# A two-layer encoder on one core: reciprocals moved in the second attention's steps, and a third token chunk of 344 columns

## The reference

```
for i in range(DEPTH):
    u = rmsnorm(h, norm_mix[i])
    mix = neighbourhood_attention(...) if kind == 0 else gqa_attention(...)
    h = h + mix
    h = h + swiglu(rmsnorm(h, norm_ffn[i]), ffn_w1[i], ffn_w3[i], ffn_w2[i])
return rmsnorm(h, norm_final)[:, N_META:]
```

## Time and profile before

| what | us |
|---|---|
| median of 3 runs (2755.27, 2755.56, 2759.28) | 2755.56 |
| the profiled execution, device time | 2760.81 |
| its span, first to last instruction | 2758.9 |
| TensorE busy in the span | 2688.9 (97%) |
| VectorE busy | 1497.9 (54%) |
| GpSimd busy | 1525.8 (55%) |
| ScalarE busy | 943.2 (34%) |
| mean granted TensorE clock | 0.993 of 2.4 GHz |

### The profile page before, as it was taken

How to read it: one execution, slowest core, us unless ns; L and a number is a source line. 1 busy time by engine, 2 the same in 40 slices (tenths; PEclk the granted TensorE clock), 3 DMA queues, 4 the chain that set the end, 5 groups by cost and what they waited for, 6 DMA issues and landing times.

```text
span 2758.9 us, 39747 instructions
## 1 busy us (share of the span) xinstructions
PE 2688.9 (97%) x14623; PEld 2209.2 (80%) x14623; DVE 1497.9 (54%) x1962; ACT 943.2 (34%) x1630; POOL 1525.8 (55%) x1291
## 2 busy tenths in 40 slices
PE   8999999899999999999999899999998999999998
PEld 7888888699999999999777444454677888888886
DVE  4444444437444444445877866767356444545545
ACT  4343343324222222223321546554232222222224
POOL 5655655445655555556344657665445555655561
PEclk9999999999999999999999999999999999999999
DMA  7221221511111111111333000001211111112111
GB/s 225 64 60 57 61 71 46 206 43 54 57 50 49 46 46 46 46 49 54 103 82 62 19 1 16 16 1 62 89 46 54 46 57 49 49 54 59 51 54 65
DMA packets 200468, 163.06 MB, mean 59 GB/s; under 512 B 19816, under 2 KB 182032, under 8 KB 200352
## 3 DMA queue, kind: packets, MB, share of 16 engines
q1 hardware_dynamic: 193728, 139.83, 17.5%
q10 hardware_dynamic: 6624, 21.68, 2.0%
HBM read 131.70 MB, written 24.51 MB: 57 GB/s over the span
## 4 chain that ended last, share of the span: by engine, by line
PE 67%; issue 11%; POOL 11%; DVE 8%; DMA 1%; ACT 1%; SPq 1%; POOLq 0%; ACTq 0%; DVEq 0%
PE PS L984 17%; PE PS L916 11%; PE PS L1035 11%; PE PS L1180 9%; POOL wl L701 6%; PE PS L1454 4%; PE PS L1468 4%; POOL upraw L695 3%; PE PS L1231 2%; DVE nmx L2530 2%; PE PS L1267 2%; PE PS L1207 2%; DVE rcp L2559 2%; PE PS L1394 2%; POOL wraw L695 1%
## 5 line engine op out<-in xcount | busy, mean ns | idle before, releaser
L701 POOL TENSOR_TENSOR wl<-upraw,wh 128x512 fp32r<-128x512 f32 x212 | 285.3, 1348 | 271.6 <-ACT wh L1587 271.2
L675 POOL TENSOR_TENSOR wh<-wraw,ones 128x512 fp32r<-128x512 f32 x120 | 140.2, 1168 | 377.2 <-PE PS L916 200.1
L2081 DVE TENSOR_TENSOR h<-PS,h 128x1044 f32<-128x1044 f32 (+1 forms) x176 | 217.1, 1234 | 198.2 <-PE PS L1035 198.1
L1587 ACT ACTIVATE wh<-upraw 128x512 fp32r<-128x512 f32 x212 | 132.7, 630 | 502.3 <-POOL upraw L695 221.2
L1954 ACT ACTIVATE pf<-PS 128x512 f32<-128x512 f32 (+1 forms) x288 | 169.9, 594 | 167.1 <-PE PS L1454 165.9
L2530 DVE TENSOR_REDUCE nmx<-PS 128x1 fp32r<-128x1044 f32 x128 | 158.3, 1240 | 113.5 <-PE PS L1394 113.4
L678 POOL TENSOR_TENSOR wl<-wraw,wh 128x512 fp32r<-128x512 f32 x120 | 191.5, 1596 | 9.4
L701 POOL TENSOR_TENSOR wl<-wraw,wh 128x512 fp32r<-128x512 f32 x74 | 98.7, 1334 | 154.3 <-ACT wh L1587 154.3
L857 POOL TENSOR_TENSOR accp<-accp,pf 128x1024 f32<-128x1024 f32 x64 | 152.0, 2376 | 19.3 <-ACT pf L1954 18.4
L1817 ACT ACTIVATE pt<-PS 128x512 f32<-128x512 f32 x128 | 75.8, 593 | 243.6 <-PE PS L1231 237.0
L1468 PE MATMUL PS<-pf,vg 128*64 128x512 f32 x576 | 156.0, 621 | 0.0
(11 more groups left out here) (342 smaller groups left out, 7298.3 us busy)
## 6 DMA issues: line engine op xcount, KB each, us to landing
upraw<-in_ffn_w SPq DMA_DIRECT2D x166, 256.0 KB, 2.8
wraw<-in_ffn_w SPq DMA_DIRECT2D x98, 256.0 KB, 2.8
wraw<-in_a_w_qkv SPq DMA_DIRECT2D x48, 256.0 KB, 2.8
biasb<-bias_shifts SPq DMA_DIRECT2D x128, 72.0 KB, 2.5
h_spill<-h ACTq DMA_DIRECT2D x16, 522.0 KB, 5.0
h<-h_spill ACTq DMA_DIRECT2D x8, 522.0 KB, 7.5
h<-h_spill SPq DMA_DIRECT2D x8, 522.0 KB, 6.9
xt<-in_x SPq DMA_DIRECT2D x16, 256.0 KB, 6.9
```

What stands on the lines that cost most here:

```text
L701: nc.gpsimd.tensor_tensor(wlr[l][slot], rb[l][r], whr[l][slot].bitcast(F32), ALU.subtract).then_inc(s_wrd, 1)
L1587: nc.scalar.activation(whr[l][(o + 1) % ring], rb[l][r], ACT.Copy).then_inc(s_xhi, 1)
L2081: nc.vector.tensor_tensor(out_, x, y, op_).then_inc(sem_, 1)
```

## The change

Four things are changed.

1. All matmuls over the third chunk of layer 0 run over `width(0, 2)` = min(348, 1040 - 696) = 344 columns, where they ran over 348. The first two chunks, layer 1 and all reads of PSUM by VectorE and ScalarE keep their widths, and so do the three matmuls for the maxima.
2. VectorE clears columns 344 to 347 of all eight PSUM banks at the start. This is a fifth increment of s_pad; the waits for it go from 4 to 5, and TensorE gets one ahead of its first transpose.
3. `o_part` is cut in two. `invert_sums` has the wait for `p_sums` and the reciprocal, `o_part` the product. Before, a half's reciprocal and product came together, in step 3 (first half) and 4 (second half). Now VectorE's list has, each behind the maxima of its step: step 1 first reciprocal, step 2 first product, step 3 second reciprocal, step 4 second product.
4. For the last block, whose output is taken after the loop, the order stays reciprocal, product, reciprocal, product.

```
 BANKS = [(NB, CW), (2, 512)]
+USED = [T, GRID]
...
-O_AT = [3, 4]
+RCP_AT = [1, 3]
+O_AT = [2, 4]
...
+def width(l, c):
+    return min(BANKS[l][1], USED[l] - BANKS[l][1] * c)
...
-                                PS[:, set_ + c, 0:cw], w, x[k][:, c * cw:(c + 1) * cw],
+                                PS[:, set_ + c, 0:width(l, c)], w, x[k][:, c * cw:c * cw + width(l, c)],
...
-                        mm = product(o1, rest[l][1], EBANK[q][1], True, False)
+                        mm = product(o1, rest[l][1], EBANK[q][1], True, False, w_=width(0, 2))
...
-                                    mm = nc.tensor.matmul(PS[:, at_[j] + e, 0:cw], w[:, w0:w0 + P],
-                                                          x[:, cw * e:cw * e + cw],
+                                    mm = nc.tensor.matmul(PS[:, at_[j] + e, 0:width(l, e)], w[:, w0:w0 + P],
+                                                          x[:, cw * e:cw * e + width(l, e)],
...
             pe.wait_ge(s_id, 16)
+            pe.wait_ge(s_pad, 5)
...
-                        mm = nc.tensor.matmul(PS[:, D0 + bk, 0:CW], w, x[c][:, bk * CW:(bk + 1) * CW],
+                        mm = nc.tensor.matmul(PS[:, D0 + bk, 0:width(0, bk)], w,
+                                              x[c][:, bk * CW:bk * CW + width(0, bk)],
...
             nc.vector.memset(h[:, :, T:TP], 0.0).then_inc(s_pad, 1)
+            nc.vector.memset(PS[:, :, width(0, 2):CW], 0.0).then_inc(s_pad, 1)
...
+            def invert_sums(n, part):
+                cols = slice(part * QB // 2, part * QB // 2 + QB // 2)
+                dve.wait_ge(s_sum, 2 * (n + 1))
+                nc.vector.reciprocal(rcp[:, cols], PS[:, 4, cols]).then_inc(s_grcp, 1)
+
             def o_part(n, part):
...
-                dve.wait_ge(s_sum, 2 * (n + 1))
-                nc.vector.reciprocal(rcp[:, cols], PS[:, 4, cols]).then_inc(s_grcp, 1)
                 dve.wait_ge(s_gpv, 2 * KT * (n + 1))
...
+                    if kt in RCP_AT and n:
+                        invert_sums(n - 1, RCP_AT.index(kt))
                     if kt in O_AT and n:
                         o_part(n - 1, O_AT.index(kt))
...
-            o_part(NBP * NG - 1, 0)
-            o_part(NBP * NG - 1, 1)
+            for part in range(2):
+                invert_sums(NBP * NG - 1, part)
+                o_part(NBP * NG - 1, part)
```

More of the change, by code:

```diff
@@ L747, in _ @@
             nc.gpsimd.memset(vt[:, :, :], 0.0).then_inc(s_vt0, 1)
-            po.wait_ge(s_pad, 4)
+            po.wait_ge(s_pad, 5)
             for n in range(4):
@@ L978, in ffn, with product @@
                 dense(ub + 6, set3, uh_, ul_, gb + 1, l)
-                def product(o, x, bank, start, stop=True):
+                def product(o, x, bank, start, stop=True, w_=cw):
                     (xh, xl), a, b = x, whr[l][(o + 1) % ring], wlr[l][(o + 1) % ring]
@@ L983, in product @@
                         for ti, (w, y) in enumerate(((a, xh), (a, xl), (b, xh))):
-                            mm = nc.tensor.matmul(PS[:, bank, 0:cw], w[:, P * k:P * k + P], y[:, k, :],
+                            mm = nc.tensor.matmul(PS[:, bank, 0:w_], w[:, P * k:P * k + P], y[:, k, 0:w_],
                                                   start=(start and k == 0 and ti == 0),
@@ L1002, in quad @@
                     if l == 0:
-                        mm = product(o2, rest[l][0], EBANK[q][0], True, False)
+                        mm = product(o2, rest[l][0], EBANK[q][0], True, False, w_=width(0, 2))
                     mm.then_inc(s_un, 1)
@@ L1006, in quad @@
                         pe.wait_ge(s_wrd, n + (o2 + 1))
-                        product(o2 + 1, rest[l][0], EBANK[q][1], False).then_inc(s_un, 1)
+                        product(o2 + 1, rest[l][0], EBANK[q][1], False, w_=width(0, 2)).then_inc(s_un, 1)
                     pe.wait_ge(s_wrd, n + o3)
@@ L1018, in quad @@
                     if l == 0:
-                        mm = product(o6, rest[l][1], EBANK[q][0], False)
+                        mm = product(o6, rest[l][1], EBANK[q][0], False, w_=width(0, 2))
                     mm.then_inc(s_un, 1)
@@ L1166, in _ @@
             pe.wait_ge(s_xra, 9)
-            pe.wait_ge(s_pad, 4)
+            pe.wait_ge(s_pad, 5)
             def filler(n, c, need):
@@ L1735, in _ @@
                           allow_slow_non_contiguous=True).then_inc(s_bfill, 16)
-            act.wait_ge(s_pad, 4)
+            act.wait_ge(s_pad, 5)
             def x_rows(i):
@@ L2265, in _ @@
             dve.wait_ge(s_const, 1)
-            dve.wait_ge(s_pad, 4)
+            dve.wait_ge(s_pad, 5)
             take_x(1, 0)
```

## The result

| what | before | after |
|---|---|---|
| median of 5 runs | 2757.69 us (2755.27 to 2759.69) | 2740.99 us (2738.35 to 2745.99) |
| profiled execution | 2760.81 | 2738.35 |
| its span | 2758.9 | 2736.6 |
| mean granted clock | 0.993 | 0.995 |

The ratio on record is 0.9933, 95% interval 0.9921 to 0.9945: 18.5 us less, 15 to 22. It isn't the quotient of the two medians above, which are 16.7 us apart. The forecast was 16.0 us less and 2739.6 us, with a range from 2736.5 to 2745.0. Two later executions, of the kernel before and of the one with the width alone, took 3612 and 3736 us at a mean granted clock of 0.68 and 0.65 and are in none of the ratios.

What follows compares the result with a forecast made beforehand. TensorE, busy for 97% of the span, was taken as the bound. Moved reciprocals (12.2 us) plus narrower third chunk (3.8) and clearing (0) gave 16.0 us off 2755.56: 2739.6 us, range 2736.5 to 2745.

Steps and rivals of the forecast that it cites:

- Where the time was lost: Second attention, blocks 1 to 14: TensorE waits 0.12 and 0.75 us for maxima queued behind reciprocals and products on DVE.
- The size of the moved reciprocals: Second attention: spreading reciprocals and products removes both old waits, 0.87 us a block, 12.2 us in 14 blocks.
- The timing of the first reciprocal: Second attention, step 2: it starts 1.10 us after the sums, DVE waits 0.18 us, TensorE keeps a 0.07 us margin.
- full-wait rival: Second attention, step 3: reciprocal starts only once step 2's maximum is ready; TensorE waits 1.03 us a block, 2754 us; chance 0.04.
- The partial wait: Second attention, step 3: first reciprocal late beyond the margin, 0.1 to 0.3 us a block returned, 2741 to 2744; chance 0.16.
- The spacing of 0.10 us everywhere: DVE in the second attention: each instruction starts 0.10 us after the last; TensorE waits about 0.1 us a block, 1.5 us less gain.
- The width: Layer 0's and layer 1's listed third-chunk matmuls: four columns save 1.66 ns each, 3.8 us in sum, between 2.9 and 4.1.
- The discount on the fillers: Neighbourhood attention: shorter fillers save nothing where TensorE waits, so 0.80 us was taken of 0.88.
- narrowing brings nothing at all: Matmul streams: pace set by more than columns, so 344 may save 0; only 12.2 us gained, 2743.4 us; chance 0.05.
- 344 columns cost more than 348: Layer 0's feed-forward network: 344 falls off the line of 348 and 512, up to +166 us, 2910; chance 0.02.
- The clearing of PSUM: Opening: memset and TensorE's wait are covered by the wait for x until 4.72; cost 0, without cover 0.1 us.
- The median: Whole kernel: 16.0 us off the three-run median of 2755.56 gives 2739.6 us.

## Why the prediction was right

**Where the time was lost: right.** TensorE waited in steps 5 and 6 of blocks 1 to 14 for a maximum behind a reciprocal and its product. With the reciprocals alone moved the waits are gone, with the width alone changed they are there.

**The size of the moved reciprocals: one term too small.** The prediction counted 0.12 + 0.75 = 0.87 us a block. The trace shows 0.96. The missing 0.10 stands in step 6: each distance that begins with matmuls that had waited is 0.10 us longer, since their weight load isn't hidden (merged rows of 0.74 to 0.75 us in place of 0.64). One such 0.10 was inside the 3.35, but the one after the last wait was in the distance from step 6 to 7, at which the prediction didn't look: 3.15 before, 3.06 after. 13.5 us and not 12.2.

**The timing of the first reciprocal: right to 0.02 us.** Forecast: 1.10 us after the sums start, a wait of 0.18. Measured: 1640.84 - 1639.73 = 1.11 and 0.19, and 1.10 with 0.19 to 0.21 in the other blocks. This was the thin place, and the full-wait rival is excluded by that row alone. The partial wait didn't come either: the margin was 0.12 in place of 0.07, because the reduction behind the reciprocal took 1.18 us and not 1.24. The spacing of DVE's instructions was as read from the earlier trace rows: the maximum starts 0.09 us before the reciprocal's recorded end (1640.84 + 1.76 against 1642.51), the product 0.08 before the maximum's. The spacing of 0.10 us everywhere, which would have cost 1.5 us, didn't come. The prediction had set it beside the Trainium skill (VectorE: DVE Perf Modes, "The DRAIN you can't avoid"), but told half of that paragraph: it also says that a next operation that is not held starts earlier. The starts of 0.08 to 0.09 us ahead agree with that half.

**The width: right in mechanism, uneven in its size.** 1.66 ns a matmul is the mean price of four columns over a wide step, not of this step: 0.4 ns in the up projections, 1.9 in the down projection, 3.2 in the fillers. Over 960, 528 and 528 matmuls that is 0.4 + 1.0 + 1.7 us, with some 0.3 for the plain projections 3.4 (3.0 by the smallest reading of the fillers), against the 3.8 of the forecast. The main part of layer 0's feed-forward network bears the first two out by its whole length, 662.96 to 662.98 us in the four profiles with 348 columns and 661.68 to 661.70 in the seven with 344: 1.3 us against their 1.4. The discount on the fillers (0.80 of 0.88) was needless. That narrowing brings nothing at all, and that 344 columns cost more than 348, are both excluded by these rows. The prediction held "the same 14 ns beside the columns at 348 and at 512" against the first of them; that was no evidence, since a line through two points has one offset by construction. By the figures of the Trainium skill (TensorE: Matmul & The Clock Gate, "Back-to-back issue gap") 32 columns would be worth 4 ns a matmul, an estimate from that page; from 344 to 312 they brought 15.6 ns in the up projections (1.50 us over 96), so those figures don't hold here.

**The clearing of PSUM: right, as far as the opening shows.** It took 0.09 us on DVE at 1.06, and the first transposes started at 4.76, released by the landing of x, against 4.72.

**The median: near, partly by luck, and part of the difference has its place in the clock.** The traces add up to 13.5 + 3.4 = 17 us. The timings say 18.5 and 19.9 (intervals from 15 to 23.5), so 17 lies inside both. The forecast of 2739.6 took its 16.0 us off a median of three executions, 2755.56; with five that median was 2757.69. The low start and the saving that came out too small pull opposite ways, and that they nearly met at 2740.99 is luck.

The width alone was measured at 5.8 and 5.2 us, with 3.4 near the low end of both intervals (3.3 and 2.8). The streams don't show the rest, but the granted clock of the timed executions does. In the rounds of the first and third sitting 42 executions with 348 columns (31 of the kernel before, 11 with the reciprocals alone) have a mean clock of 0.9920, and one of them 0.994 or more. The 28 with 344 columns (22 with the width alone, 6 of the changed kernel) have 0.9932, and 13 of them 0.994 or more; both sittings show it. The reciprocals alone don't raise it (0.9918). By 0.0012 of the clock an execution of 2757 us has 6.6 us less at half clock, worth at most 3.3 us. Among executions of one kernel, those with 0.001 more of clock are 1.6 us shorter on the average. That gives about 2 us, an estimate that fits the excess of 2.4 and 1.8. So the width does go with fewer stretches at half clock; why isn't shown. The prediction put this at nothing: "Nothing in my terms lies in what differs between them".

## What to carry to other kernels

Where one engine's short, steady turns release another engine, and the same queue also has long instructions, spread the long ones so that never more than one stands between two turns: the same 4.3 us of work cost 0.96 us a block in two lumps and nothing in four pieces. Walk the queue with durations from one block before moving anything; it gave each new start in the changed kernel to 0.1 us here, and told the free orders from those that cost something, though one cost came out twice too large. Look at the granted clock of all timed executions beside their times: here it held 2 us that no stream showed. For trimming a few columns of a matmul, take the price from a stretch of the stream itself: over four columns it went from 0.4 to 3.2 ns with the surroundings.

## What the runs showed of the hardware

- A wait of TensorE costs its length and 0.10 us more for the weight load behind it, even where the wait itself is 0.02 to 0.03 us (2.64, then 2.72). A weight load that is held up while its matmul still comes in time costs nothing (2.61 us, load 0.12 us ahead instead of 0.22).
- A reduction of 128 x 1044 takes 1.18 us right behind a reciprocal (28 of 28 in blocks 1 to 14 of the changed kernel) and 1.22 to 1.25 otherwise.
- A reciprocal of 256 columns takes 1.75 us, of 512 columns 3.36.
- A DVE instruction that waits for nothing starts 0.07 to 0.09 us ahead of the recorded end of the one before.
- Stretches of a few microseconds with TensorE's clock at 1.2 GHz in place of 2.4 stand at other places in each profile of one program: block 0 of the second attention had none in one profile of the reciprocals alone and some in the next. After the same wait of TensorE for DVE (1.65 us) the clock fell at 1529 in the execution before (0.83 in the mean over 20 us) and not in the changed kernel's (1.00).
- Executions with 344 columns in the third chunk had a mean granted clock of 0.9932, those with 348 columns 0.9920.
